# Index scores split around the first softmax maximum, with their products in a room of their own

## What is computed

```python
proj = rmsnorm(x, g_pre_mix) @ w_in          # 3404 columns: q, k, v of four kinds of attention
# kind A: each query picks 64 keys by an index score, then softmax over those
dots  = einsum('bthd,bsd->bths', iq, ik)     # 8 index heads
score = einsum('bth,bths->bts', iw, relu(dots)) + causal
_, idx = top_k(score, 64)
# kind B: forgetting attention, kind C: differential, kind D: sliding window with sinks
```

## Time and profile before

| | us |
|---|---|
| median of 3 runs | 1958.08 (1957.68 to 1962.58) |
| the profiled execution | 1962.05, span 1960.2 |
| PE busy in it | 1887.3 (96%), mean clock 0.984 |
| DVE busy | 1169.7 (60%) |
| ACT busy | 885.6 (45%) |
| POOL busy | 92.6 (5%) |

### The profile page before, as it was taken

How to read it: one execution, slowest core, us unless ns; L and a number is a source line. 1 busy time by engine, 2 the same in 40 slices (tenths; PEclk the granted TensorE clock), 3 DMA queues, 4 the chain that set the end, 5 groups by cost and what they waited for, 6 DMA issues and landing times.

```text
span 1960.2 us, 23117 instructions
## 1 busy us (share of the span) xinstructions
PE 1887.3 (96%) x9135; PEld 1553.6 (79%) x9135; DVE 1169.7 (60%) x1360; ACT 885.6 (45%) x1071; POOL 92.6 (5%) x108
## 2 busy tenths in 40 slices
PE   7989999999899999999999999998999999999997
PEld 5877888878778888888877778886888877778885
DVE  5785555657765557456576574556456576574555
ACT  5544444655354435444345443443444345443442
POOL 6310000021200000000000000000000000000000
PEclk9988999999899999999999999999999999999998
DMA  8414655543765555663555645556663556645552
GB/s 254 146 46 133 193 184 169 204 162 124 105 203 193 183 172 213 204 216 100 166 172 199 219 150 181 184 185 210 207 215 98 169 169 208 211 151 183 184 187 89
DMA packets 194385, 340.17 MB, mean 174 GB/s; under 512 B 9342, under 2 KB 59422, under 8 KB 194304
## 3 DMA queue, kind: packets, MB, share of 16 engines
q1 hardware_dynamic: 189072, 327.76, 51.0%
q0 software_dynamic: 5232, 11.29, 3.2%
HBM read 333.24 MB, written 5.77 MB: 173 GB/s over the span
## 4 chain that ended last, share of the span: by engine, by line
PE 86%; DVE 7%; ACT 3%; DVEq 2%; issue 1%; DMA 0%; SPq 0%; ACTq 0%
PE G L647 19%; PE G L648 19%; PE G L652 18%; PE T L700 5%; PE A L647 4%; PE A L648 4%; PE A L652 4%; PE G L662 2%; PE G L663 2%; PE G L668 2%; PE A L759 1%; DVE wlo L1606 1%; PE T L749 1%; PE A L662 1%; ACT whi L1154 1%
## 5 line engine op out<-in xcount | busy, mean ns | idle before, releaser
L1606 DVE TENSOR_TENSOR wlo<-raw,whi 128x2048 fp32r<-128x2048 f32 (+3 forms) x300 | 630.3, 2103 | 570.3 <-ACT whi L1154 570.1
L1154 ACT ACTIVATE whi<-raw 128x2048 fp32r<-128x2048 f32 (+3 forms) x300 | 527.1, 1759 | 587.8 <-PE G L652 512.9
L647 PE MATMUL G<-whi,XH 128*128 128x512 f32 (+1 forms) x1408 | 560.4, 398 | 7.6 <-DVE XL L1620 6.3
L648 PE MATMUL G<-whi,XL 128*128 128x512 f32 (+1 forms) x1408 | 549.6, 390 | 0.0
L652 PE MATMUL G<-wlo,XH 128*128 128x512 f32 (+1 forms) x1408 | 346.2, 388 | 0.0
L647 PEld LDWEIGHTS G<-whi,XH 128*128 128x128 f32 x1408 | 266.1, 189 | 64.3 <-DVE XL L1620 8.0
L648 PEld LDWEIGHTS G<-whi,XL 128*128 128x128 f32 x1408 | 266.3, 189 | 53.8 <-issue 1.9
L652 PEld LDWEIGHTS G<-wlo,XH 128*128 128x128 f32 x1408 | 264.0, 188 | 53.6
L700 PE MATMUL T<-ident,arena 128*128 128x128 f32 x804 | 114.8, 282 | 19.6 <-ACT arena L1154 10.9
L700 PEld LDWEIGHTS T<-ident,arena 128*128 128x128 f32 x804 | 94.6, 144 | 38.2 <-issue 11.8
L1154 ACT ACTIVATE arena<-T 128x512 f32<-128x512 f32 (+2 forms) x92 | 45.9, 549 | 157.5 <-PE T L700 157.4
(11 more groups left out here) (237 smaller groups left out, 2236.9 us busy)
## 6 DMA issues: line engine op xcount, KB each, us to landing
raw<-in_w_in SPq DMA_DIRECT2D x112, 1024.0 KB, 7.3
raw<-in_w_mlp_up SPq DMA_DIRECT2D x32, 1024.0 KB, 5.3
raw<-in_w_mlp_down SPq DMA_DIRECT2D x32, 1024.0 KB, 5.0
raw<-in_w_ffn_gate SPq DMA_DIRECT2D x44, 512.0 KB, 4.1
raw<-in_w_ffn_up SPq DMA_DIRECT2D x44, 512.0 KB, 5.1
raw<-in_w_ffn_down SPq DMA_DIRECT2D x44, 512.0 KB, 3.7
raw<-in_w_out SPq DMA_DIRECT2D x16, 1024.0 KB, 4.9
raw<-in_w_ret_proj SPq DMA_DIRECT2D x16, 1024.0 KB, 5.0
```

The source lines that it names most:

```text
L647: nc.tensor.matmul(dst(m), hx[:, k0 + k, rows], hi[:, k, :], start=first and k == 0, stop=False)
L648: nc.tensor.matmul(dst(m), lx[:, k0 + k, rows], hi[:, k, :], start=False, stop=False)
L1154: return nc.scalar.activation(out_, in_, func, **kw)
L1606: tt(lo_, raw[:, slot, 0:n], hi.bitcast(F32), ALU.subtract).then_inc(part_sem(blk, c, s_lo, s_lo1), 1)
```

## The change

`RL` moves from 12952 to 10904 in the arena, so that it no longer covers `PR` but the blocks 13 to 20 of `QT`, which hold the turned queries and keys of kinds C and D and are written in steps 2 and later. `scores` gets a first and an end head. `scores(1)` before the jobs stops after head 4; heads 5, 6, 7 and the causal mask follow in `beside(0)`, after `prep` of job 0 and ahead of `lo` of unit 13. This holds for both layers of the first block.

```diff
-        RL = room(12952, IDX_HEADS, S)
+        RL = room(10904, IDX_HEADS, S)
...
-                def scores(m):
+                def scores(m, first=0, end=IDX_HEADS):
                     n = (m + 1) * P
                     sc = SCO[:, 0:n]
                     dve.drain()
                     dve.wait_ge(s_rl.sem, s_rl.at(0, L, 1 + 2 * m))
-                    ts(sc, RL[:, 0, 0:n], IW[:, m, 0:1], None, ALU.mult)
-                    for h in range(1, IDX_HEADS):
+                    if first == 0:
+                        ts(sc, RL[:, 0, 0:n], IW[:, m, 0:1], None, ALU.mult)
+                    for h in range(max(1, first), end):
                         dve.drain()
                         ins = stt(out=sc, in0=RL[:, h, 0:n], scalar=IW[:, m, h:h + 1], in1=sc, op0=ALU.mult, op1=ALU.add)
+                    if end < IDX_HEADS:
+                        return
                     ins.then_inc(s_rlf.sem, 1)
                     dve.drain()
                     tt(sc, sc, causal[:, m, 0:n], ALU.add)
...
-                scores(1)
+                scores(1, 0, 5)
 
                 def beside(q):
 
                     if q == 0:
+
+                        scores(1, 5)
                         lo(0, L, 0, 13)
```

## The result

The change made the kernel **slower by 0.52%**: the median went from 1961.59 us (22 runs, 1956.17 to 1968.62) to 1972.42 us (22 runs, 1965.83 to 1981.13), ratio 1.0052 with a 95% interval of 1.0040 to 1.0063. The ratio is worth 10.2 us, the two medians lie 10.8 apart; the text goes by the ratio. The three runs that the prediction had give 1958.08 and lie low in the spread of the 22. The profiled execution has a span of 1971.3 us against 1960.2.

What follows compares the result with a forecast made beforehand. The prediction took PE, busy for 96% of the span, as the bound, reachable only in the first block's attention. DVE's low part 2.0 us late in each of 2 layers gave +4.0 us, hence 1962.1 us, range 1957.2 to 1967.5.

Steps and rivals of the forecast that it cites:

- the sum: Total for the first block's attention: 2 layers x 2.0 = +4.0 us, giving 1962.1 us; chance 0.58.
- the second rival: PE's new idle time before the kind C turns and turn of job 1 brings half clock: 9.4 us, 1967.5; chance 0.19.
- The sign that the prediction had named: A slower PE clock anywhere between 104 and 124 us would make the prediction wrong.
- The term that was worked out: On DVE, one head passes per POOL instruction, so the low part of unit 13 starts 2.0 us late per layer.
- sharing: DVE and POOL share traffic, about 0.35 us per meeting: low part 1.3 us late, 1960.7; chance 0.21 together with no blocking.
- Part 2: Earlier maximum of job 0: its exponentials start 1.88 us earlier, PE gains at most 0.5 us and can't keep it.
- Part 4: Effect on PE: kind C turns start 0.7 us later, turn of job 1 at 110.84 instead of 108.82.
- Rival 1: DVE's heads slip between POOL's instructions: -0.45 us per layer, 1957.2; chance 0.21 together with sharing.
- Rival 3: ACT's 1.88 us or PE's 0.5 us reaches the end: 1.0 us gained, 1957.1; chance 0.01 for over 0.3%.

Runs made afterwards that it cites:

- run 2: Kernel before, with four unused maxima (2.0 us of DVE delay per layer meant) ahead of the low part of unit 13; ratio 1.0049 to the kernel before.
- run 3: Changed kernel with unused matmuls meant for PE's two new waits, the second group misplaced so only the first wait was filled; ratio 1.0037 to the kernel before.
- run 5: Changed kernel with both of PE's new waits filled by unused matmuls, the second group now placed in its wait; ratio 1.0028 to the kernel before.
- run 8: Kernel before, with PE's four longest late attention waits filled by unused matmuls in both layers; ratio 0.9956 to the kernel before, repeated 0.9954.
- run 9: Changed kernel with its two new waits and the four late waits of PE filled by unused matmuls; ratio 0.9989 to the kernel before, 1960.43 us.
- run 4: Changed kernel with POOL's rotation of the kind C keys held back until DVE's low part of unit 13; ratio 1.0010 to the kernel before.
- run 1: Kernel before with only `RL` moved to 10904, the scores in one piece; ratio 0.9993 to the kernel before, 1959.15 us.
- run 6: Changed kernel with the split after head 6, so only head 7 and the mask add follow the maximum; ratio 1.0045 to the kernel before.
- run 7: Kernel before, with two unused maxima (1.0 us of DVE delay per layer meant) ahead of the low part of unit 13; ratio 1.0045 to the kernel before.

## Why the prediction was wrong

**The time lies outside the range** of 1957.2 to 1967.5, and the change is slower by over 0.3%, which had a chance of 0.19. The step that failed is the sum, which priced PE's new idle time at nothing beyond its own length. The turn of job 1 came 4.3 us late in the two layers together and the loss was 10.2 (7.8 to 12.4), so that term was about 6 us and not 0. Not all of the distance to the range is that: the 22 runs put the kernel before 3.5 us higher than the three did. What stood as the second rival is what happened: its sum of 9.4 us is within 1 us of the 10.2 measured, and 9.4 on the median of 22 runs would have been 1971.0. I gave it too small a chance. That its number is so near is in part luck, since its 2.7 us per layer came from one late turn of one execution, and the two layers of the changed kernel lost 2.3 and 5.6 us beyond their delay. The sign that the prediction had named, a slower clock between 104 and 124 us, is in the profile: 0.91 over the window from 106 us. The row for this rival was there: the wait of 1.92 us at 144.10 and the half clock behind it. I had found no row that says where new spells fall, and did not ask what a wait of 1.8 us would do 35 us earlier.

What the runs show of this term: run 2 gets the loss from a delay alone; runs 3 and 5 lose 7.3 and 5.5 us for 8.2 and 4.3 us of delay once waits are filled; and in the first layers of runs 8 and 9, with the clock at 1.00 throughout, 2.28 us of delay cost 2.28 us. Together they show that waits of PE here cost more than their length and that the half clock behind them is the rest. No single ratio shows it: the intervals of run 5 and of the changed kernel overlap. The Trainium skill, TensorE: Matmul & The Clock Gate, Part 1, says that the throttled state is the default and that activity releases it. The filled runs agree: 41 us at half clock in the kernel before, 6 with the late waits filled.

**The term that was worked out held to 0.05 us.** Laid out by turns between DVE and POOL, the low part of unit 13 was put at 2.0 us late; it is 1.99 and 1.97. Each head came where the list had it (the profile is shifted by 0.24: heads 5, 6, 7 end at 95.64, 97.08, 98.49 against 95.89, 97.33, 98.77 less 0.24). Run 4 shows that POOL is the cause, run 1 that the room is not. The reading that the later engine stands still for the whole of the other's instruction gave this sum; sharing would have given 1.3. The Trainium skill, SBUF — State Buffer, section "SBUF: two separate sides", states that reading as a rule, and the 2.0 us agree with it.

**Part 2** held but for a size: `nm` at 94.70, exponentials at 95.18. PE gained 0.67 us at the turn of job 0 (98.84 less 97.93 less 0.24) and not at most 0.5, because the sum took PE as busy to the modelled end of its last matmul, and the turn started 0.17 us before that end. The gain was gone at the kind C turns, as forecast. **Part 4** held: kind C turns at 104.14 (104.3 forecast, less 0.24), turn of job 1 at 110.88 (110.84 less 0.24, and 0.3 us on top in the first layer, where DVE has a gap of 0.31 in its own issue that it had not before).

**Rival 1**, DVE slipping between POOL's instructions, did not happen, even where run 6 came within 0.04 us of it. **Rival 3**, a gain, had 0.01.

What stays open: how the 6 us divide over the single waits. Run 5 removes the first fall of the clock and loses 4.7 us less than the changed kernel (1.0028 against 1.0052, intervals that overlap at 1.0040 to 1.0047). Half-clock time is left in later stretches, whose moments move from one profiled execution to the next. The time that delay and issue gaps cost in runs 2 and 7 could not be set to a wanted dose.

## What to carry to other kernels

Moving work behind a maximum moves it into other company: before splitting a DVE sequence, list which GpSimd instructions run beside its new place, and compare the ends of instructions, since an instruction that stands still ends a fixed time after the one that blocks it. Ask of every new wait of TensorE, also of one that comes only because TensorE arrives earlier, what follows it at full clock today; and where TensorE waits anyway, matmuls that nobody reads can be worth more than they cost. A head start for an engine that is not the last to arrive gives nothing, however large its idle time looks.

## What the runs showed of the hardware

- A DVE instruction over SBUF of 0.17 us (4 values per partition) or 0.48 us (256, two inputs) that started behind one of GpSimd's `rope` instructions took 0.48 to 0.66 us or 0.78 to 1.53 us and ended 0.02 or 0.27 to 0.29 us after it. The maximum over PSUM took its usual 0.68 beside line 628, and in run 4 the picks (`MAX8`, `MATCH_REPLACE8`) took their usual 0.43 and 0.41 beside lines 625 to 628, which took 0.73, 0.73 and 1.27.
- In the changed kernel GpSimd started lines 628 and 630 0.14 us after its last end and 0.21 us ahead of the head that this end had released, in both layers. In the kernel before DVE's low part came 0.2 us ahead of line 630, which then took 2.46 us instead of 1.27.
- Read in rows of 2 us, TensorE's clock is 0.50 or 1.00 (1.2 or 2.4 GHz), with values between only at the edges of a stretch. Waits of 1.34 and 2.02 us in the first layer were followed by half clock, and the same stretch with 12 unused matmuls in these waits ran at 1.00. With the first of the two filled and the second left it ran at 1.00 as well (run 3), and a wait of 1.26 us alone had half clock behind it (run 4).
- Forty-six unused matmuls (23 per layer) took 0.45% off the time.
- Executions with late fillers show a stop of 1.2 to 3.6 us in TensorE's issue in the second layer, where the DMA queue of GpSimd is at about 90%; the two plain kernels' profiles, with the queue as busy (89.9% and 90.5%), show no such stop.
